# Stick-breaking encoder layer: two slots of a steady step issued together on TensorE

## The reference, cut to what matters

```
z = einsum('bhqd,bhkd->bhqk', q, k) * scale
before = key index < query index
log_stay = where(before, log_sigmoid(-z), 0)
log_pass = reverse_cumsum(log_stay) - log_stay
a = where(before, exp(log_sigmoid(z) + log_pass), 0)
out = einsum('bhqk,bhkd->bhqd', a, v)
```

## Time and profile before

| what | value |
|---|---|
| median of three runs | 1358.17 us |
| the profiled execution, its own time | 1356.08 us |
| its span in the trace | 1354.3 us |
| TensorE (PE) busy | 1318.5 us, 97% |
| DVE busy | 709.6 us, 52% |
| ACT busy | 541.3 us, 40% |
| POOL busy | 331.1 us, 24% |
| mean granted TensorE clock | 0.993 |

### The profile page before, as it was taken

The page is one execution under the profiler, slowest core; times in us unless marked ns, Lnnn a source line. Parts: engine busy times, 40 slices in busy tenths (PEclk is TensorE's granted clock), DMA queues, the critical chain, the costliest instruction groups (busy, mean ns, idle before and its releaser), DMA issues.

```text
span 1354.3 us, 18027 instructions
## 1 busy us (share of the span) xinstructions
PE 1318.5 (97%) x6648; PEld 1113.3 (82%) x6648; DVE 709.6 (52%) x880; ACT 541.3 (40%) x964; POOL 331.1 (24%) x229
## 2 busy tenths in 40 slices
PE   6999999999999988999999999999999999999998
PEld 6888888888888876788888888888888888888886
DVE  7699989898998997435104131313122222223227
ACT  5667767677777774334221211121202121111122
POOL 2111011101101000553441424232423232323332
PEclk9999999999999998999999999999999999999999
DMA  5000000000000004310110202021111111111112
GB/s 217 17 31 32 17 32 32 15 31 31 16 31 31 16 1 140 106 66 31 32 65 29 78 16 77 22 71 40 53 46 62 43 50 46 46 47 47 47 47 109
DMA packets 18340, 66.72 MB, mean 49 GB/s; under 512 B 2032, under 2 KB 2032, under 8 KB 18288
## 3 DMA queue, kind: packets, MB, share of 16 engines
q1 hardware_dynamic: 16704, 60.30, 13.1%
q10 hardware_dynamic: 1584, 5.77, 1.3%
HBM read 61.87 MB, written 4.19 MB: 49 GB/s over the span
## 4 chain that ended last, share of the span: by engine, by line
PE 91%; DVE 5%; ACT 2%; DMA 1%; POOL 1%; issue 1%; SPq 0%; DVEq 0%; POOLq 0%; ACTq 0%
PE bank L1288 12%; PE bank L1286 12%; PE bank L1284 12%; PE bank L1126 6%; PE bank L1127 6%; PE bank L1128 6%; PE bank L1351 5%; PE bank L1352 5%; PE bank L1353 5%; PE bank L1226 4%; PE bank L1200 3%; PE bank L1202 2%; PE bank L1246 2%; PE bank L1245 2%; PE bank L1174 2%; PE bank L1175 2%
## 5 line engine op out<-in xcount | busy, mean ns | idle before, releaser
L741 POOL TENSOR_TENSOR w_lo<-raw,w_hi 128x1024 fp32r<-128x1024 f32 x86 | 209.4, 2439 | 823.2 <-ACT w_hi L461 822.9
L1284 PE MATMUL bank<-hnT_hi,w_hi 128*128 128x512 f32 (+1 forms) x712 | 275.5, 387 | 0.0
L1288 PE MATMUL bank<-hnT_hi,w_lo 128*128 128x512 f32 (+1 forms) x712 | 275.3, 387 | 0.0
L1286 PE MATMUL bank<-hnT_lo,w_hi 128*128 128x512 f32 (+1 forms) x712 | 275.3, 387 | 0.0
L1031 DVE TENSOR_TENSOR sg<-bank,sg 128x512 f32<-128x512 f32 x44 | 30.4, 691 | 428.1 <-ACT sg L672 428.1
L461 ACT ACTIVATE w_hi<-raw 128x1024 fp32r<-128x1024 f32 x88 | 92.3, 1059 | 394.9 <-PE bank L1288 344.2
L936 DVE TENSOR_TENSOR_SCAN stay<-stay,diag_one 128x256 f32<-128x256 f32 (+7 forms) x128 | 180.2, 1408 | 3.7 <-ACT stay L575 3.7
L1286 PEld LDWEIGHTS bank<-hnT_lo,w_hi 128*128 128x128 f32 x712 | 133.7, 188 | 27.1
L1288 PEld LDWEIGHTS bank<-hnT_hi,w_lo 128*128 128x128 f32 x712 | 133.7, 188 | 27.1
L1284 PEld LDWEIGHTS bank<-hnT_hi,w_hi 128*128 128x128 f32 x712 | 133.7, 188 | 27.1
L1045 DVE TENSOR_TENSOR y<-bank,y 128x512 f32<-128x512 f32 x160 | 108.3, 689 | 82.5 <-PE bank L1353 75.4
(11 more groups left out here) (117 smaller groups left out, 2113.4 us busy)
## 6 DMA issues: line engine op xcount, KB each, us to landing
raw<-in_units SPq DMA_DIRECT2D x98, 512.0 KB, 3.2
acc<-in_x SPq DMA_DIRECT2D x8, 512.0 KB, 9.6
x_in<-in_x ACTq DMA_DIRECT2D x8, 512.0 KB, 3.4
out<-y SPq DMA_DIRECT2D x7, 512.0 KB, 2.6
g_pre_s<-in_mix_pre SPq DMA_DIRECT2D x1, 512.0 KB, 5.2
g_post_t<-in_mix_post ACTq DMA_DIRECT2D x1, 512.0 KB, 4.5
g_ffn_t<-in_ffn_pre ACTq DMA_DIRECT2D x1, 512.0 KB, 4.9
g_out<-in_ffn_post ACTq DMA_DIRECT2D x1, 512.0 KB, 3.5
```

Source lines behind the costliest of these rows:

```text
L741: nc.gpsimd.tensor_tensor(w_lo[slot], raw[:, raw_slot, :], w_hi[slot].bitcast(F32), ALU.subtract).then_inc(w_ready, 1)
L1284: nc.tensor.matmul(dst, wh, hnT_hi[:, kt, cols], start=(kt == 0 and b == 0), stop=False, skip_group_check=halves > 1)
L1286: nc.tensor.matmul(dst, wh, hnT_lo[:, kt, cols], start=False, stop=False, skip_group_check=halves > 1)
L1288: mm = nc.tensor.matmul(dst, wl, hnT_hi[:, kt, cols], start=False, stop=last, skip_group_check=halves > 1)
```

## The change

A table `DOUBLE` names eight even slots: with the slot behind each, slots 0 to 5 and 10 to 19. The slot's body is cut into three functions, `step_values`, `step_transposes` and `step_scores`, whose text is that of before with the same waits. In the six steady steps (not in step 0, step 7 and the tail) TensorE issues for such a pair of slots s, s+1: values of s, values of s+1, the first projection part of s, transposes of s, transposes of s+1, scores of s, scores of s+1, then the pair's other parts in their old order. Slots 6 to 9 keep the order of before. ACT, DVE, POOL and SP are untouched.

```
+DOUBLE = (0, 2, 4, 10, 12, 14, 16, 18)
...
+            def step_values(p, s, first, tail):
...
+                    pe.wait_ge(t_lo, t_index(p + dp, g) + 1)
...
+            def step_transposes(p, s, first, tail):
...
+                        pe.wait_ge(t_lo, g - 1)
...
+                        pe.wait_ge(row_done, 16 * p + 4 * group + T_CHUNKS[x][c][0] + 2)
...
+            def step_scores(p, par, s, first):
...
+                    pe.wait_ge(sig_done, z - 1)
...
             def step(p, par, first=False, proj=True, slots=SLOTS):
                 tail = slots < SLOTS
                 for s in range(slots):
 
...
+                    if not first and proj and s in DOUBLE:
+                        for u in (s, s + 1):
+                            step_values(p, u, first, tail)
+                        fill(p, par, first, fill_parts(s, first)[0], proj)
+                        for u in (s, s + 1):
+                            step_transposes(p, u, first, tail)
+                        for u in (s, s + 1):
+                            step_scores(p, par, u, first)
+                        for part in (fill_parts(s, first)[1], *fill_parts(s + 1, first)):
+                            fill(p, par, first, part, proj)
+                        continue
+                    if not first and proj and s - 1 in DOUBLE:
+                        continue
+                    step_values(p, s, first, tail)
                     if not tail:
                         fill(p, par, first, fill_parts(s, first)[0], proj)
...
+                    step_transposes(p, s, first, tail)
                     if not tail:
...
+                        step_scores(p, par, s, first)
                         fill(p, par, first, fill_parts(s, first)[1], proj)
```

More of the change, by code:

```diff
@@ L1178, in wo_part @@
                     mm.then_inc(mix_full, 1)
+            def step_values(p, s, first, tail):
+                dp, at = (0, s - AV_LAG) if s >= AV_LAG else (-1, s - AV_LAG + SLOTS)
+                if not (first and s < T_LAG + AV_LAG) and not (tail and s >= T_LAG + AV_LAG):
+                    z = (at - T_LAG) % SLOTS
+                    h, x = GROUPS[z // GROUP]
+                    g = next(n for n, kind, _ in t_slot(at) if kind == "a")
+                    group = 4 * (p - (s < T_LAG + AV_LAG)) + z // GROUP
+                    if z % GROUP == 0 and not (isinstance(group, int) and group < 2):
+                        pe.wait_ge(o_done, group - 1)
+                    pe.wait_ge(t_lo, t_index(p + dp, g) + 1)
+                    blocks_, _ = t_blocks(x, z % GROUP)
+                    for m, (j, ks, c0) in enumerate(blocks_):
+                        w = P * len(ks)
+                        dst = OB[h][:, P * ks[0]:P * ks[0] + w]
+                        v = V[:, j, 2 * h:2 * h + 2, :].rearrange("p a c -> p (a c)")
+                        hi, lo = AT_hi[:, (s - T_LAG) % 2, c0:c0 + w], AT_lo[:, (s - T_LAG) % 2, c0:c0 + w]
+                        nc.tensor.matmul(dst, v, hi, start=(z % GROUP == 0 and m == 0), stop=False,
+                                         skip_group_check=True)
+                        mm = nc.tensor.matmul(dst, v, lo, start=False, stop=(z % GROUP == GROUP - 1 and m == 1),
+                                              skip_group_check=True)
+                    mm.then_inc(av_done, 1)
@@ new lines, in step_transposes @@
+            def step_transposes(p, s, first, tail):
+                for n, kind, at in t_slot(s):
+                    g = t_index(p, n)
+                    if kind == "v" and not tail:
+                        pe.wait_ge(t_lo, g - 1)
+                        pe.wait_ge(acc_free, acc_base(p) + 1 + at)
+                        for q in range(4):
+                            mm = nc.tensor.transpose(TB[(n - T_LAG) % 2][:, q * P:(q + 1) * P],
+                                                     vT[:, q * P:(q + 1) * P], ident[:, :])
+                        mm.then_inc(t_full, 1)
+                    elif kind == "a" and not (first and s < T_LAG) and not (tail and s >= T_LAG):
+                        pe.wait_ge(t_lo, g - 1)
+                        group, c = divmod(at, GROUP)
+                        h, x = GROUPS[group]
+                        group -= 4 if s < T_LAG else 0
+                        pe.wait_ge(row_done, 16 * p + 4 * group + T_CHUNKS[x][c][0] + 2)
+                        for j, ks, c0 in t_blocks(x, c)[0]:
+                            for q, k in enumerate(ks):
+                                src = ROW_OFF[x][k] + P * (j - ROWS[x][k])
+                                mm = nc.tensor.transpose(TB[(n - T_LAG) % 2][:, c0 + q * P:c0 + (q + 1) * P],
+                                                         A[:, h, src:src + P], ident[:, :])
+                        mm.then_inc(t_full, 1)
@@ new lines, in step_scores @@
+            def step_scores(p, par, s, first):
+                n, c = divmod(s, GROUP)
+                h, x = GROUPS[n]
+                z = SLOTS * p + s
+                if s == 0:
+                    pe.wait_ge(acc_free, acc_base(p) - (0 if first else 1))
+                if s == SLOTS // 2:
+                    pe.wait_ge(acc_free, acc_base(p))
+                if not (isinstance(z, int) and z < 2):
+                    pe.wait_ge(sig_done, z - 1)
+                kk = k_tile(h, par)
+                parts = z_parts(x, c)
+                for m, (r, a, e, c0, c1) in enumerate(parts):
+                    dst = ZB[s % 2][:, c0 - Z_COLS[c][0]:c1 - Z_COLS[c][0]]
+                    qs = slice(Q_POS[r] * P, (Q_POS[r] + 1) * P)
+                    nc.tensor.matmul(dst, q_hi2[:, h, qs], kk[:, a:e], start=True, stop=False)
+                    mm = nc.tensor.matmul(dst, q_lo2[:, h, qs], kk[:, a:e], start=False, stop=True)
+                mm.then_inc(z_full, 1)
@@ L1182, in step @@
                 for s in range(slots):
[L1184 to L1204, removed]
@@ L1229, in step @@
-                    if not tail:
[L1230 to L1247, removed]
+                    step_transposes(p, s, first, tail)
```

## The result

The kernel after takes 1420.68 us (median; 1418.19 to 1420.90), the kernel before 1358.16 us: ratio 1.0464, 95% interval 1.0451 to 1.0477. It is slower by 62.5 us. The forecast was 1408 us in a range from 1390 to 1424.

A forecast was written before the change was run, and what follows sets the result against it. TensorE, full in the steady steps with feeders close behind, bounds the kernel. Stalls of 7.1 us a step (43 us over six) plus 7 us of clock give 1406, forecast 1408 us with the runs' median offset; range 1390 to 1424.

The forecast's parts named there:

- rival 4: Steady steps: the clock falls twice in a step, after the stalls of 3.3 and 2.1 us: 1421 us; chance 0.12.
- What bounds the kernel, and no gain from the order: Steady steps: TensorE is always busy, its feeders close behind; issuing pairs in another order removes no instruction and no wait.
- The stall at slot 3, 3.3 us: Pair 0, 1 into 2, 3: TensorE waits 3.3 us for AT_lo of slot 1, behind the q copies.
- the lower bound: Slot 3: with DVE's times left where they are, the stall is 2.4 us.
- Slot 5, 0 us: Pair 2, 3 into 4, 5: no stall, between 0 and 2.3 us, as the stall before has paid for it.
- Slots 13 and 17, 2.1 and 1.4 us: Stalls for AT_lo of slots 11 and 15: 2.1 us behind k copies, 1.4 us behind ACT's copies and weight split.
- Slot 1, 0.3 us: Pair 18, 19 into 0, 1: stall of 0.3 us for AT_lo of slot 19, between 0 and 0.7.
- The clock, 7 us: Steady steps: one fall to half clock a step, 3.4 us long, at 1.2 us each; 7 us, between 0 and 20.
- The first: Rival, steady steps: TensorE's clock stays up, 1401 us; chance 0.18.
- The second: Rival, joined pairs: the order saves switches of 0.08 us a pair and the leads suffice, 1354 us; chance 0.03.
- The fifth: Rival: the change does not act because the pairs' conditions are never met, 1358 us; chance 0.02.
- the third: Rival: ACT and DVE catch up more, only the stall behind the q copies stays, 1378 us; chance 0.08.

The follow-up runs named there:

- e1: Kernel after with only the pairs of slots 10, 14 and 18 joined (18 of the 48): 1357.05 us, ratio 1.0001 to the kernel before.
- e4: Kernel after with the q copies of slot 0 and k copies of slots 10 and 14 done one slot later: 1386.06 us, ratio 1.0214.
- e9: Kernel after, but transposes and scores of s stand ahead of those of s+1, values still together: 1406.72 us, ratio 1.0373.
- e5: Kernel after with slots 0 and 1 taken one by one: 1404.99 us, ratio 1.0358 to the kernel before.
- e2: Kernel after with only the pair 2, 3 joined: 1376.84 us, ratio 1.0149 to the kernel before.
- e3: Kernel after with 25 extra matmuls a step in the stalls (12 at slot 3, 8 at slot 13, 5 at slot 17): 1401.29 us, ratio 1.0320.
- e6: Kernel after with the 12 extra matmuls at slot 3 only, stalls at slots 13 and 17 left empty: 1404.29 us, ratio 1.0345.

## Why the prediction was right, step by step

The waits came as walked. The time of 1408 us is 12.7 too low, and the clock's term is nearly all of it: 7 us were taken for it, and it cost 19.5. That 1420.68 is still inside the range is owed to the range's upper end, which was set by rival 4 and not by the forecast.

- **What bounds the kernel, and no gain from the order.** Right: e1 has pairs without stalls and keeps the time.
- **The stall at slot 3, 3.3 us.** Measured 3.22 idle (3.4 from start to start). The chain runs as walked: 8.81 us to the end of AT_lo of slot 1 for 8.72. e4 takes the q copies out of it and the stall falls to 0.2; e9 takes the 0.44 out and it falls by 0.43; e5 and e2 give the lower bound, 2.3 for 2.4.
- **Slot 5, 0 us.** Right: no wait there. AT_lo of slot 3 ends 5.86 us after the values of slot 3 (329.83 - 323.97) for 5.9, 0.22 us before it is wanted. The prediction took the 5.97 us between two AT_lo from the rows without saying what is in them. 2.2 us of it are DVE held by POOL, in both kernels: the multiplication takes 2.75 us beside w_lo (at 323.83; before, at 289.35, 2.77), and 0.55 in e4, where w_lo comes later. First POOL's row of the kernel after, then DVE's of e4:

```profile
323.78 2.38 POOL L743 TENSOR_TENSOR w_lo<-raw,w_hi 128x1024 fp32r<-128x1024 f32 x1 [19.99 <-ACT w_hi L463]
```

```profile
301.43 0.55 DVE L942 TENSOR_TENSOR A<-A,stay 128x384 f32<-128x384 f32 x1
```
- **Slots 13 and 17, 2.1 and 1.4 us.** Measured 1.98 and 1.28 idle. At slot 13 AT_lo ends 7.97 us after the pair's first values (348.71 to 356.68) for 7.95. The size is right and the path only half: the walk took the k copies as what comes last and did not look at DVE's rows, and that these end at about the same time (e9) was luck. e4 shows that moving the copies still helps, since k_lo stands ahead of AT_lo on DVE as well.
- **Slot 1, 0.3 us.** In the steady state 0.1 or less is booked as idle, 0.2 from start to start; 0.65 in the first step, whose step before is not joined, as the bound of 0.7 had it.
- **Sum of the waits, 43 us.** Measured 43.4 (six times the step at full clock), and 44.0 in e3. Nothing was won back: step 7 takes 47.97 us, and took 47.96 before.
- **The clock, 7 us.** This is the mis-sized term: 19.5 us. The prediction had one fall of 3.4 us a step at 1.2 us. In the trace there are 44.4 us at half clock in the six steps: three steps with 10.2 us, two with 6.8, one with none. Two things were missed. In five steps it also falls behind the stall at slot 13, as rival 4 has it with its 1421 us. And behind slot 3 it stays down for 6.8 us in three steps, of which this is one:

```profile
245.00:250.00 5.00, 3.98 (x22) 3.23 (x20) 2.70 (x5) 4.41 (x9) 0.00 (x0) 1.00 0.00 0
250.00:255.00 5.00, 2.79 (x10) 2.40 (x11) 4.75 (x5) 1.94 (x4) 2.36 (x1) 0.58 0.00 0
255.00:260.00 5.00, 5.00 (x21) 4.40 (x20) 4.05 (x4) 2.83 (x6) 0.00 (x0) 0.74 0.32 107
```

The stall at slot 3 lasts from 249.0 to 252.2; the clock is then low, in part, up to 257.6, over work that fills TensorE. The price of 1.2 us for 3.4 was also low: 19.5 us for 44.4 is 0.44 per us at half clock, 1.5 us for 3.4, and e2's steps show 1.6.
- **The Trainium skill's 275 ns for a transpose** (TensorE: Matmul & The Clock Gate, Part 4: PE-mode transpose). As the duration of one it agrees: seven that start 0.11 us apart take 0.93 us, which leaves 0.27 for the last. Seven transposes and the step to the score take 0.68 us here (316.37 to 317.05), six spacings of 0.11 and 0.02 more. For a set the spacing was the right price, and e9's 0.43 us for four confirms it.
- **Rivals.** The first (clock stays up, 1401) is what e3 makes true by other means, at 1401.3. The second fell with e1, whose 18 pairs give nothing back. The fifth fell with the waits themselves, the third too: slots 13 and 17 wait in every step. The fourth (1421) came closest: five steps have two falls. That its number fits so well is in part chance, since one step has no fall and in three steps one of the two lasts 6.8 us.

## What to carry to other kernels

An engine that is full and an engine that feeds it with half a microsecond of lead are one machine: before two slots are joined, walk the feeder's queue in its own order and add up what stands in it (copies, splits, additions), and do so for the pair ahead as well. Price an idle stretch of TensorE at more than its length: in the kernel after each us of stall cost 1.45 us, 0.45 of it in clock. In e4, where no stall of the steady state is over 1.7 us, the clock fell in one step of six only. Where a wait can't be removed, matmuls that compute nothing, put into a bank that is about to be overwritten, gave the clock's part back.

## What the runs showed of the hardware

- TensorE's clock fell behind single stalls between full work, and not behind each: behind 2.3 us (e2, four steps of six), 2.0 us (e6 at slot 13, two steps of six) and 1.7 us (e4 at slot 5, one step of six). In the kernel after it fell in five steps of six, behind the stall at slot 3 and again behind that at slot 13; in the fourth step the same stalls of 3.22, 1.98 and 1.28 us left it at 1.00. With 25 extra matmuls a step (e3) it stayed at 1.00 in all six steps; with 12 of them, 2.8 us, in the stall at slot 3 (e6) it no longer fell there. Why the same stalls bring it down in one step and not in another is not shown by these runs.
- A DVE scan with both inputs in SBUF took 3.62 us beside POOL's 2.42 us w_lo and 2.28 us without it, while DVE's AT_lo, with one input in PSUM, took 0.56 us in both cases. The Trainium skill has this as a lock (SBUF — State Buffer, Who interferes with whom): a DVE instruction with two SBUF inputs and a GpSimd one that reads SBUF block each other. The trace agrees, with 1.3 us of delay where 1.5 us of w_lo were left when the scan could start (305.23 to 306.70). In the kernel after, where w_lo starts first too, DVE's multiplication with two SBUF inputs takes 2.75 us (323.83), and 0.55 in e4, where w_lo is not beside it.
